# Experts' loop of a hybrid decoder layer: the small block's rows are turned ahead of its down unit, from one buffer

## What is computed

```python
def expert_block(args):
    xb, e = args
    return (jax.nn.silu(xb @ w_g[e]) * (xb @ w_u[e])) @ w_d[e]

ybuf = lax.map(expert_block, (xbuf.reshape(n_blocks, MOE_BLK, D_MODEL), block_e))
y = ybuf.reshape(n_blocks * MOE_BLK, D_MODEL)[dest] * gate_s[:, None].astype(xt.dtype)
return jax.ops.segment_sum(y, tok_s, num_segments=n_tok)
```

## Time and profile before

| | us |
|---|---|
| median of 3 runs | 2663.48 (2662.52 to 2665.42) |
| the profiled execution | 2664.51 |
| its span, first to last instruction | 2662.9 |
| TensorE matmuls busy | 2536.5 (95%) |
| VectorE busy | 1763.0 (66%) |
| ScalarE busy | 1604.8 (60%) |
| GpSimd busy | 865.0 (32%) |
| mean DMA rate | 190 GB/s |

### The profile page before, as it was taken

How to read it: one execution, slowest core, us unless ns; L and a number is a source line. 1 busy time by engine, 2 the same in 40 slices (tenths; PEclk the granted TensorE clock), 3 DMA queues, 4 the chain that set the end, 5 groups by cost and what they waited for, 6 DMA issues and landing times.

```text
span 2662.9 us, 59695 instructions
## 1 busy us (share of the span) xinstructions
PE 2536.5 (95%) x19448; PEld 1779.8 (67%) x19449; DVE 1763.0 (66%) x3617; ACT 1604.8 (60%) x2613; POOL 865.0 (32%) x948
## 2 busy tenths in 40 slices
PE   5899999999999999999389999999999999999996
PEld 2345555555555555555178888888888888888885
DVE  5677777777777777777645556655665565556643
ACT  7565556555665556555356667766776665567742
POOL 1132323332233323332133433344334343343332
PEclk9899999999999999999689999999999999999998
DMA  9376666666666666666757778877887768588852
GB/s 312 90 170 153 159 148 166 159 158 154 155 170 150 164 150 162 164 157 148 221 163 230 217 234 266 254 202 234 265 255 202 247 190 246 161 245 267 249 134 49
DMA packets 550283, 507.24 MB, mean 190 GB/s; under 512 B 412779, under 2 KB 412940, under 8 KB 549212
## 3 DMA queue, kind: packets, MB, share of 16 engines
q1 hardware_dynamic: 517372, 405.56, 53.2%
q0 software_dynamic: 32720, 100.60, 15.8%
q10 hardware_dynamic: 144, 0.52, 0.0%
HBM read 322.09 MB, written 87.36 MB: 154 GB/s over the span
## 4 chain that ended last, share of the span: by engine, by line
PE 88%; DVE 3%; DMA 3%; issue 2%; ACT 2%; POOL 1%; SPq 1%; DVEq 0%; POOLq 0%; ACTq 0%
PE psG L611 11%; PE psG L1932 8%; PE psH L1932 8%; PE psA L1894 8%; PE psB L1894 8%; PE psC L1894 6%; PE psE L611 6%; PE psF L611 6%; PE psD L611 6%; PE psC L611 6%; PE psD L1894 5%; PE psH L611 3%; PE psE L1925 1%; DMA wo_all<-in_w_out 1%; DMA wi_all<-in_w_in 1%
## 5 line engine op out<-in xcount | busy, mean ns | idle before, releaser
L611 PE MATMUL psG<-wi_all,both_xT 128*128 128x512 f16 x1536 | 345.9, 381 | 3.5 <-DVE qsq L1402 3.5
L611 PEld LDWEIGHTS psG<-wi_all,both_xT 128*128 128x128 f16 x1536 | 148.6, 98 | 180.3 <-issue 8.9
L2025 ACT ACTIVATE unread<-wi_all 128x4096 fp8e4<-128x4096 f32 x62 | 223.6, 3606 | 0.0
L1809 POOL COPY scatter_rows<-pending 128x1 int32<-128x1 int32 x79 | 66.9, 846 | 480.7 <-DVE y L2172 313.9
L872 ACT ACTIVATE prob<-prob,soft,s_stat 128x256 f32<-128x256 f32 x256 | 150.6, 589 | 97.7 <-DVE soft L1295 97.5
L611 PE MATMUL psE<-wo_all,both_mT 128*128 128x512 f16 x768 | 179.8, 384 | 3.4 <-DMA both_mT<-prob 3.2
L611 PE MATMUL psF<-wo_all,both_mT 128*128 128x512 f16 x768 | 176.2, 379 | 0.0
L2158 DVE SCALAR_TENSOR_TENSOR gate_lo<-wi_all,own,gate_hi 128x2048 f16<-128x2048 f32 x64 | 150.2, 2347 | 38.6 <-ACT gate_hi L2029 32.6
L2158 DVE SCALAR_TENSOR_TENSOR up_lo<-wi_all,own,up_hi 128x2048 f16<-128x2048 f32 x64 | 147.6, 2348 | 35.5 <-issue 32.1
L611 PE MATMUL psC<-wi_all,both_xT 128*128 128x512 f16 x768 | 171.0, 379 | 0.0
L611 PE MATMUL psD<-wi_all,both_xT 128*128 128x512 f16 x768 | 171.0, 379 | 0.0
(11 more groups left out here) (406 smaller groups left out, 7463.3 us busy)
## 6 DMA issues: line engine op xcount, KB each, us to landing
wi_all<-in_w_gate SPq DMA_DIRECT2D x32, 2048.0 KB
wi_all<-in_w_up SPq DMA_DIRECT2D x32, 2048.0 KB, 10.1
wi_all<-in_w_down SPq DMA_DIRECT2D x32, 2048.0 KB
um<-u_rows SPq DMA_DIRECT2D x64, 256.0 KB, 2.8
out_rows<-h SPq DMA_DIRECT2D x32, 512.0 KB, 2.9
xt<-in_x SPq DMA_DIRECT2D x31, 512.0 KB, 3.8
xres<-in_x SPq DMA_DIRECT2D x31, 512.0 KB, 4.7
hn_rows<-xres SPq DMA_DIRECT2D x31, 512.0 KB, 2.9
```

The lines of the kernel that those rows point to most:

```text
L611: m = nc.tensor.matmul(ps, left[:, l, k, :], weights.half(r, k, n, width), start=(k == opens and j == 0), stop=(k == closes and j == 2))
L1809: g.tensor_copy(scatter_rows[s][:], pending[:, s, 0:1]).then_inc(named, 1)
L2025: s_.activation(unread[:].bitcast(mybir.dt.float8e4), w, ACT.Abs, accum_out=sums(p, n), saturate=False).then_inc(summed, 1)
```

## The change

The first small rows and those of further blocks share one buffer, `xgt`, with one semaphore, `tail_rows_in`. An expert without a small block turns no small rows. In an expert with one, the turn stands at the head of `tail`, then comes the down unit, then the small block's gate and up. The gather of the next small block's rows is issued at the head of GpSimd's `tail`, and that of the next expert's first small rows in `close`, after the last scatter. The buffers are no longer filled with zeros. The down unit waits for the low parts of the activations in two halves everywhere, and so the small block's are made in two halves. `turned` counts 4 for each expert, and `halves` counts the low parts.

```diff
+    xgt = sb("xgt", [P, D])
-    def turned(e, t):
-        return 5 * e + 4 + t
+    def halves(e, t):
+        return 2 * e + 2 * t
+    def turned(e, t):
+        return 4 * e + 4 + t
...
         def big(e, p, r, t, ahead):                                # GpSimd
             if ahead:
                 pool.wait_ge(listed_in, 32 * E if ahead == 1 else 32 * (e + 3))
-            pool.wait_ge(first_in, 16 * (e + 1))
-            if not is_zero(e):
-                pool.wait_ge(more_in, 16 * (e + t))
-                pool.wait_ge(xT_ps, turned(e, t) - 4)
+            pool.wait_ge(tail_rows_in, 16 * (e + t + 1))
...
-            gather_tail(xg_more, more, more_in)
             if ahead > 2:
                 load_lists(e + 3)
-            if ahead:
-                pool.wait_ge(xT_ps, turned(e, t) + 1)
-                hold(pool, held)
-                gather_tail(xg_first, first_rows, first_in)
 
         def tail(e, p, t, i):
+            pool.wait_ge(xT_ps, turned(e, t) + 1)
+            hold(pool, held)
+            gather_tail(more)
             scatter(2 * e + t, 0)
...
-            pool.wait_ge(more_in, 16 * (e + t + 1))
+            pool.wait_ge(tail_rows_in, 16 * (e + t + 2))
             hold(pool, held)
             pool.dma_start(more[0:TAIL, :], table[...]).then_inc(tail_in, 16)
-            pool.wait_ge(xT_ps, turned(e, t) + 2)
             pool.wait_ge(tail_in, 16 * (t + 1))
             hold(pool, held)
-            gather_tail(xg_more, more, more_in)
...
             scatter(2 * e + t + 1, 0)                              # close
             if ahead:
+                pool.wait_ge(tail_rows_in, 16 * (e + t + 1))
+                hold(pool, held)
+                gather_tail(first_rows)
                 pend(e + 1, listed(e + 1, t))
...
-        pool.wait_ge(cleared, 5)
+        pool.wait_ge(cleared, 3)
...
-        def down(d, s):
+        def down(d, s, ready):                                     # TensorE
             pe.wait_ge(y_act, d + 1)
-            down_part(psG, 0, s, range(KE)).then_inc(y_ps, 1)
+            pe.wait_ge(aT_lo_s, ready + 1)
+            down_part(psG, 0, s, (0, 1))
+            pe.wait_ge(aT_lo_s, ready + 2)
+            down_part(psG, 0, s, (2, 3)).then_inc(y_ps, 1)
...
             rows_times((psA, psB), gate_ps, "gate")
-            turn_tail(xg_first, first_in, e + 1)
...
         def tail(e, t):
+            pe.wait_ge(xT_lo, turned(e, t))
+            turn_tail(e + t + 1)
+            pe.wait_ge(lo_s["down"], CHUNKS * (e + 1))
+            down(2 * e + t, 0, halves(e, t))
             pe.wait_ge(xT_lo, turned(e, t) + 1)
             pe.wait_ge(silu_s, parts(e + 1, t))
             tail_times(psA, gate_ps, "gate")
             pe.wait_ge(prod_s, parts(e + 1, t))
             tail_times(psB, up_ps, "up")
-            turn_tail(xg_more, more_in, e + t + 1)
-            pe.wait_ge(lo_s["down"], CHUNKS * (e + 1))
-            pe.wait_ge(aT_lo_s, parts(e + 1, t))
-            down(2 * e + t, 0)
...
         def tail(e, p, t, i):                                      # ScalarE
-            act.wait_ge(gate_ps, parts(e + 1, t) + 1)
-            act.wait_ge(aT_lo_s, parts(e + 1, t))
-            s_.activation(act_of_tail[:], psA[:, 0:KE * TAIL], ACT.Silu, ...)
-            turn_tail(turned(e, t) + 2)
+            turn_tail(turned(e, t) + 1)
             act.wait_ge(added, emptied(2 * e + t))
             copy_y(2 * e + t, 0, listed(e, t) + 2)
+            act.wait_ge(gate_ps, parts(e + 1, t) + 1)
+            act.wait_ge(aT_lo_s, halves(e + 1, t))
+            s_.activation(act_of_tail[:], psA[:, 0:KE * TAIL], ACT.Silu, ...)
...
         def tail(e, p, t, i):                                      # VectorE
+            turn_tail(turned(e, t) + 1)
+            dve.wait_ge(added, emptied(2 * e + t))
+            copy_y(2 * e + t, 0, listed(e, t) + 2)
             dve.wait_ge(up_ps, parts(e + 1, t) + 1)
...
-            v.tensor_tensor(aT_lo[:, :, 0:TAIL], ..., ALU.subtract).then_inc(aT_lo_s, 1)
+            for pair in (slice(0, 2), slice(2, 4)):
+                v.tensor_tensor(aT_lo[:, pair, 0:TAIL], ..., ALU.subtract).then_inc(aT_lo_s, 1)
...
-        for rows in (xg_first, xg_more):
-            v.memset(rows[:], 0.0).then_inc(cleared, 1)
```

More of the change, by code:

```diff
@@ L1657, in experts @@
     y = [sb(f"y_{s}", [P, D]) for s in range(2)]
-    xg_first, xg_more = sb("xg_first", [P, D]), sb("xg_more", [P, D])
+    xgt = sb("xgt", [P, D])
     gT_hi, gT_lo = sb("gT_hi", [P, KD, BIG], F16), sb("gT_lo", [P, KD, BIG], F16)
@@ L1696, in experts @@
     chosen, named, pending_s = sem("chosen"), sem("named"), sem("pending_s")
-    rows_in, first_in, more_in, added = sem("rows_in"), sem("first_in"), sem("more_in"), sem("added")
+    rows_in, tail_rows_in, added = sem("rows_in"), sem("tail_rows_in"), sem("added")
     xT_ps, xT_hi, xT_lo = sem("xT_ps"), sem("xT_hi"), sem("xT_lo")
@@ L1796, in tail_of, with gather_tail @@
             return tail_lists[:, bass.ds(e, 1), i].rearrange("p o w -> p (o w)")
-        def gather_tail(rows, listing, signal):
-            pool.indirect_dma_start(rows[0:TAIL, :], None, hn_dram, bass.IndirectOffsetOnAxis(ap=listing[0:TAIL, 0:1], axis=0),
-                                    bounds_check=SEQ + P - 1).then_inc(signal, 16)
+        def gather_tail(listing):
+            pool.indirect_dma_start(xgt[0:TAIL, :], None, hn_dram, bass.IndirectOffsetOnAxis(ap=listing[0:TAIL, 0:1], axis=0),
+                                    bounds_check=SEQ + P - 1).then_inc(tail_rows_in, 16)
         def scatter(d, s):
@@ L1849, in tail @@
             pool.wait_ge(pending_s, listed(e, t) + 5)
-            pool.wait_ge(more_in, 16 * (e + t + 1))
+            pool.wait_ge(tail_rows_in, 16 * (e + t + 2))
             hold(pool, held)
             pool.dma_start(more[0:TAIL, :], table[bass.ds(e * CAP + BIG + (i + 2) * TAIL, TAIL), :]).then_inc(tail_in, 16)
-            pool.wait_ge(xT_ps, turned(e, t) + 2)
             pool.wait_ge(tail_in, 16 * (t + 1))
             hold(pool, held)
-            gather_tail(xg_more, more, more_in)
         def close(e, p, r, t0, t, ahead):
             if ahead > 1:
-                pool.wait_ge(xT_ps, turned(e, t) + 3)
+                pool.wait_ge(xT_ps, turned(e, t) + 2)
                 gather(e + 2, 0)
@@ L1863, in close @@
             if ahead > 1:
-                pool.wait_ge(xT_ps, turned(e, t) + 5)
+                pool.wait_ge(xT_ps, turned(e, t) + 4)
                 gather(e + 2, 1)
@@ L1918, in turn_half, with turn_tail @@
             m.then_inc(xT_ps, 1)
-        def turn_tail(rows, landed, number):
-            pe.wait_ge(landed, 16 * number)
+        def turn_tail(number):
+            pe.wait_ge(tail_rows_in, 16 * number)
             hold(pe, held)
             for c in range(KD):
-                m = nc.tensor.transpose(psE[:, c * TAIL:(c + 1) * TAIL], rows[0:TAIL, c * P:(c + 1) * P], ident[0:TAIL, 0:TAIL])
+                m = nc.tensor.transpose(psE[:, c * TAIL:(c + 1) * TAIL], xgt[0:TAIL, c * P:(c + 1) * P], ident[0:TAIL, 0:TAIL])
             m.then_inc(xT_ps, 1)
@@ L1963, in tail @@
             tail_times(psB, up_ps, "up")
-            turn_tail(xg_more, more_in, e + t + 1)
-            pe.wait_ge(lo_s["down"], CHUNKS * (e + 1))
-            pe.wait_ge(aT_lo_s, parts(e + 1, t))
-            down(2 * e + t, 0)
         def close(e, t0, t):
             if not is_last(e):
-                pe.wait_ge(xT_lo, turned(e, t) + 1)
+                pe.wait_ge(xT_lo, turned(e, t))
                 pe.wait_ge(rows_in, 32 * (e + 2))
@@ L1980, in close @@
             pe.wait_ge(lo_s["down"], CHUNKS * (e + 1))
[L1981 to L1989, removed]
+            down(2 * e + t, 1, halves(e, t0))
+            down(2 * e + t + 1, 0, halves(e, t))
         def expert(e):
@@ L2066, in big @@
                 act.wait_ge(y_ps, 2 * parts(e, t))
-                act.wait_ge(aT_lo_s, parts(e, t))
+                act.wait_ge(aT_lo_s, halves(e, t))
             for c in range(CHUNKS):
@@ L2075, in big @@
                 sum_up("gate", e + 1, 1 - p, r + p, 2 * e + 3)
-            turn_tail(turned(e, t) + 1)
             for h in range(2):
@@ L2080, in tail @@
         def tail(e, p, t, i):
-            act.wait_ge(gate_ps, parts(e + 1, t) + 1)
-            act.wait_ge(aT_lo_s, parts(e + 1, t))
-            s_.activation(act_of_tail[:], psA[:, 0:KE * TAIL], ACT.Silu, scale=inverse(p, "gate")).then_inc(silu_s, 1)
-            turn_tail(turned(e, t) + 2)
+            turn_tail(turned(e, t) + 1)
             act.wait_ge(added, emptied(2 * e + t))
             copy_y(2 * e + t, 0, listed(e, t) + 2)
+            act.wait_ge(gate_ps, parts(e + 1, t) + 1)
+            act.wait_ge(aT_lo_s, halves(e + 1, t))
+            s_.activation(act_of_tail[:], psA[:, 0:KE * TAIL], ACT.Silu, scale=inverse(p, "gate")).then_inc(silu_s, 1)
             act.wait_ge(prod_s, parts(e + 1, t) + 1)
@@ L2095, in close @@
                 upper("gate", 1 - p, 0)
```

(12 more changed lines are left out.)

## The result

The changed kernel takes 2683.7 us (median of 6 runs, 2682.0 to 2688.41) where the kernel before, run beside it, takes 2663.0. The ratio is 1.0077, with a 95% interval of 1.0065 to 1.009: 20.7 us slower. The likeliest value of the forecast was 2667.2, 3.7 us above before. The result lies inside the stated range (2641 to 2692), and the place of the loss that the forecast named was the right one, but the loss was sized too small.

The account below looks back on a forecast made before the run. TensorE's own issue time was taken as the bound. Turns -12.6, first expert -0.4, start -2.1, moved units -8.4, waits +21.8 and clock +5.4 gave +3.7 us on 2663.48, so 2667.2; range 2641 to 2692.

Parts of the forecast that it names:

- The turns: On TensorE, 17 experts without a small block lose the turn between gate and up, 0.74 us each: 12.6 us saved.
- The fills: At the start, without two zero fills of gather buffers, the first list load begins 2.1 us earlier.
- The move of the turn and the down unit: In 15 experts, both go ahead of the small block's gate and up: -0.6 us each on TensorE.
- The gather behind the scatter: At the small block's head TensorE waits 1.9 or 1.3 us, rows landing 10.6 us after scatter issue: +21.8 us.
- the odd experts: After an expert without small block, their last scatter goes out 12.5 us after gate's start, 11.9 in even ones.
- rival (c): GpSimd stays late after an expert with a small block, 8 of 14 wait 1.3 us more: 2685; chance 0.1.
- a wait of over 2.5 us: Sign in the profile, before the small block's turn on TensorE, that would point to rival (c).
- The number of waits: TensorE waits for the gather in 14 experts with a small block, 6 odd and 8 even, the first excluded.
- The clock: After 6 in 10 of six long waits TensorE's clock falls, 1.5 us each: 5.4 us, bounds 0 and 21.
- the one observed case: After a single 1.8 us stall TensorE's clock was 0.50, and the down product took 4.45 us, usually 2.95.
- Rival (b): The wait is 1.9 us in all 14 small blocks, each with 1.5 us of clock: 2687.6; chance 0.2.
- Rival (a): The gather is in time at the small block, only 0.2 us waits are paid: 2642.8; chance 0.22.

Follow-up runs that it names:

- e4: The kernel of e1 with 8 transposes of 64 rows put back between gate and up of each of the 32 big blocks: 2666.2 us, ratio 1.0009.
- e5: The kernel before without the two zero fills at the start, nothing else changed: 2662.65 us against 2665.8, ratio 0.9985.
- e1: The changed kernel with the gather of the next expert's first small rows issued ahead of the last scatter, not behind it: 2640.8 us, ratio 0.9913.
- e7: The kernel of e1 with the halves of each small block's down unit in the order they become ready: 2635.6 us, ratio 0.9884.
- e3: The changed kernel with 16 extra matmuls (1.75 us) ahead of each small block's turn, where TensorE waits for the gather: 2674.5 us, ratio 1.0039.
- e2: The changed kernel with the gather issued immediately ahead of the last scatter's transfer, after that scatter's waits and list copy: 2641.6 us, ratio 0.9916.
- e8: The changed kernel with the gather held back until the last scatter has landed: 2745.7 us, ratio 1.0301.

## Why the prediction was right and wrong

**The turns, 12.6 us: right.** Gate to gate went from 34.89 to 34.16, the predicted 34.15, and e4 priced a turn at 0.73 for 0.74.

**The fills, 2.1 us: right in place, and right in size as far as it can be told.** From the small instruction of VectorE to the first list load it is 3.0 us before and 0.9 in e5 and in the changed kernel, which is the 2.1. In the sum of the changed kernel's profile it can't be seen, since the mixer ended some 3.4 us later in that execution and hid it (the first gate product starts at 1347.7 against 1347.9).

**The move of the turn and the down unit, -0.6: right where the turn waits, too good where it doesn't.** In the changed kernel the interval of 48.33 us holds a wait of 2.50, so 45.8 without it, 0.6 below 46.4. In e1 the wait for the activations was 0.3 and not 0.2 and cost some 0.6 (e7), and the interval is 46.4: nearly nothing is gained. e7 gave 46.0.

**The gather behind the scatter: the mechanism was right, the size was not, and this is the step that failed.** The last scatter goes out at G + 12.5 in odd experts and G + 11.9 in even ones, nearly as predicted (in experts 1 and 29, odd ones, it leaves at G + 12.0 and 11.9; expert 29 had done so before as well, so "the odd experts" in the prediction was not exact). The experts after one with a small block are no longer late, as argued against rival (c). But the rows are usable 11.6 us after that scatter's issue (2118.67 to 2130.31), not 10.6. The window of q0 in the changed kernel from 2123.4 to 2127.7, and the next to 2129.4, show two of the three parts (packets, MB, share):

```profile
q0 software_dynamic: 155, 0.57, 63.6%
...
q0 software_dynamic: 68, 0.22, 42.5%
```

The scatter's 144 packets are through by about 2127.7, 9.0 after issue as in the earlier trace rows, and the gather's rows begin as they end. These then took 1.5 us and not the 1.2 that half of the earlier trace rows gave, and from the last of them to TensorE another 1.1. Here I chose 0.4, by the argument that the 1.1 us of GpSimd's row held steps of its own; that row was the nearest one, its value was the right one, and it was my upper bound. With 11.6 the waits come out at 2.9 and 2.3 us, as measured (2.9 to 3.2 in the odd experts, 2.4 to 2.6 in the even ones; 2.8 in expert 29 and 3.2 in expert 1, whose gathers took 10.0 and 10.2 us and not 9.6). 13 waits of 2.8 are 36.2 us for the 21.8 of the sum. The prediction also took a wait of over 2.5 us as the sign of (c); ten of the 13 are longer, and (c) is not what happened.

**The number of waits: 13 and not 14.** In the small block of expert 30 the scatter left at 2597.41, 7.6 us after the gate's start, since the one before it landed in some 6.5 us, where others take 10 to 11. What the trace shows to differ there is the weight loads on the hardware queue q1. The queue (packets, MB, share) and the scatter (us from issue to landing) in two windows, from 2105.1 to 2115.5, ahead of expert 19, and from 2588.6 to 2595, ahead of expert 30, where q1 has no packet:

```profile
q1 hardware_dynamic: 1002, 2.05, 61.3%
...
out_rows<-y,scatter_rows POOLq DMA_INDIRECT x1, 10.4
```

```profile
q0 software_dynamic: 225, 0.86, 69.0%
...
out_rows<-y,scatter_rows POOLq DMA_INDIRECT x1, 6.3
```

The gather behind the last scatter of all, at 2646.9, has no packet of q1 beside it either and lands in 5.4 us; it goes out 3.0 us after its scatter, the others 1.9.

Over the changed kernel's loop, 20 of the 79 scatters have no packet of q1 between issue and landing and land in 6.0 to 7.3 us; of the other 59, 58 take 9.3 to 10.8. So the weight loads beside these transfers are likely a part of the 11.6. The prediction has no term for them and no experiment moved them, so their share is not shown.

**The clock: right in kind, three times too small.** The sum had 5.4 us, from a chance of 6 in 10 at six waits near 1.9 us. The waits were longer and all of them could lose it: 8 of 13 did, each for 3.4 or 6.8 us at the lower level and at a cost of 1.6 or 2.9 to 3.0 us. That is 17.0 us in the profiled execution; e3 puts it at some 15 for the median. The profiled execution was 4.7 us slower than the median, which would fit with more falls than usual; there is a trace of this one only. The prediction also had more to go by than "the one observed case": in the kernel before, a second wait, 1.94 us in the last expert, was followed by 3.4 us at the lower level. Rival (b), a wait of 1.9 and 1.5 us of clock in all 14 places, has 2687.6 and lies nearer to the result than the forecast. That nearness is in part luck: its waits were too short (26.6 us for 36.2), its falls too many (14 for 8), and the two errors offset each other.

With the measured terms the sum closes for the profiled execution. The turns give -12.3 and, in the last expert, -0.7. In the 13 experts that wait, an interval without wait and clock is 45.84 us after and was 46.51 on average before, -8.8 in all (the prediction's -0.6 each would be -7.8); the waits give +36.2 and the clock +17.0. Against this the single stall of 1.8 us and its fall of the clock are gone, -3.6; the start gives -0.2; and the last expert is another 3.6 us shorter, of which 1.7 is the fall of the clock named above, and the rest, 1.9 us, is not explained. Together +24 where the span grew by 23.9.

**Rival (a)**, the gather in time, gave 2642.8 from the same terms. It is what e1 and e2 measured when the gather was moved: 2640.8 and 2641.6. The rule that spoke for it, in the Trainium skill's page "DMA: Bandwidth & Descriptors" (the section on the anatomy of one DMA), gives an estimate of 2.6 us for such a gather; alone in its queue it took 4.0 (e8), and with the scatter ahead 9.6. The same page of the Trainium skill says in its section "Two DMAs through the same engine are not ordered" that within one queue of one DMA engine descriptors start in order, though they are pipelined. The traces agree with that rule: the gather's rows begin as the scatter's packets end, and it took 7.1 us ahead of the scatter and 9.6 behind it.

## What to carry to other kernels

When a buffer is given up, ask where the transfer that used it will now be issued and what stands ahead of it in its queue, and add the issue, the queue and the landing up to the time at which the data is due. Here one line put ahead of another turned a loss of 0.8% into a gain of 0.9%. Where a term of a few tenths of a microsecond decides the sign and is paid in 14 places, take the nearest row's value and not a smaller one argued from it; ask of every time read from a trace what the other queues moved beside it; and count for every new wait of TensorE of some 2 us that it may bring the lower clock with it.

## What the runs showed of the hardware

The same gather of 64 rows on the software queue took 4 us from issue to landing when alone behind a landed scatter (e8), 7.1 us ahead of a scatter at G + 12 (e2), 9.6 us behind it (the changed kernel), and 11.1 us behind a scatter and a gather of 128 rows (e1). In e8 and in e2 nothing stood ahead of it in its queue; a difference between them is the load on q1 meanwhile, 0.5 MB at the median in e8 and 2.2 MB in e2. In e2 the last two such gathers, with 0.1 MB or nothing on q1, took 4.9 and 5.1 us. Waiting for the scatter to land before issuing the gather delayed the issue by 8.3 us but the landing by only 2.8.

In these runs the length of a wait alone does not tell whether TensorE's granted clock falls. With waits of 2.42, 2.54, 2.83, 2.87, 3.00, 3.04 and 3.19 us (twice) it went to the lower level; with 2.44, 2.50, 2.57 (twice) and 3.11 us it did not. With the waits of 0.8 to 1.4 us in e3 it fell in one place of 13, and with the 13 of 5.0 to 6.5 us in e8 it fell every time, in 12 of them before the wait had ended. Of waits between, 1.84 and 1.94 us in the kernel before had a fall, and 1.48 us in e8 and 1.90 us in the changed kernel had none.
